# Computing the relative-position bias rows in TensorE's opening instead of behind the first chunk

## The reference

```python
for i in range(2):
    x = layer_norm(ALPHA * x + 0.5 * swiglu(x, w_gate[i, 0], w_up[i, 0], w_down[i, 0]), ...)
    m = mixer_attention(x, ...) if i == 0 else mixer_sgu(x, ...)
    x = layer_norm(ALPHA * x + m, ...)
    x = layer_norm(ALPHA * x + 0.5 * swiglu(x, w_gate[i, 1], w_up[i, 1], w_down[i, 1]), ...)
    x = x + sigmoid(x @ ple_w_gate[i]) * (p[i] @ ple_w_proj[i])
```

```python
s_own = q @ k.T * scale + rel_bias.T[head, t5_bucket(t - s)]    # 32 buckets, 8 heads; s <= t only
```

## Time and profile before

| | us |
|---|---|
| median of 3 runs | 1002.44 (1002.22 to 1002.56) |
| the profiled execution | 1002.16 |
| its span, first to last instruction | 1000.4 |
| TensorE busy | 992.9 |
| VectorE busy | 705.2 |
| ScalarE busy | 458.3 |
| GpSimd busy | 44.7 |

### The profile page before, as it was taken

How to read it: one execution, slowest core, us unless ns; L and a number is a source line. 1 busy time by engine, 2 the same in 40 slices (tenths; PEclk the granted TensorE clock), 3 DMA queues, 4 the chain that set the end, 5 groups by cost and what they waited for, 6 DMA issues and landing times.

```text
span 1000.4 us, 13938 instructions
## 1 busy us (share of the span) xinstructions
PE 992.9 (99%) x5372; PEld 849.6 (85%) x5372; DVE 705.2 (70%) x875; ACT 458.3 (46%) x523; POOL 44.7 (4%) x57
## 2 busy tenths in 40 slices
PE   9999999999999999999999999999999999999998
PEld 7888888879877888888888888888898888888887
DVE  5866666778678766666786766667787876666684
ACT  5444344246564553434355443434354553434441
POOL 0500000100001000000010000000210000000010
PEclk9999999999999999999999999999999999999999
DMA  8965656456236676565547756565467676565631
GB/s 286 286 228 170 211 171 214 131 177 201 85 127 204 217 233 213 170 213 171 175 162 254 239 173 213 169 215 175 150 191 236 212 236 214 169 213 169 215 128 43
DMA packets 129831, 191.51 MB, mean 191 GB/s; under 512 B 5464, under 2 KB 95832, under 8 KB 129792
## 3 DMA queue, kind: packets, MB, share of 16 engines
q1 hardware_dynamic: 126432, 180.11, 54.6%
q0 software_dynamic: 3072, 10.61, 3.0%
q10 hardware_dynamic: 288, 0.26, 0.1%
HBM read 189.90 MB, written 1.06 MB: 191 GB/s over the span
## 4 chain that ended last, share of the span: by engine, by line
PE 94%; DVE 3%; DMA 1%; ACT 1%; issue 0%; SPq 0%; DVEq 0%; ACTq 0%
PE gu L599 26%; PE gu L607 14%; PE acc L417 9%; PE acc L418 9%; PE acc L419 9%; PE gu L417 5%; PE gu L419 5%; PE gu L418 5%; PE tp L512 2%; PE gu L813 2%; PE gu L901 2%; DVE g_lo L1294 1%; PE gu L794 1%; PE gu L818 1%; PE gu L906 1%; DMA rawA<-in_ffn_w_up 1%
## 5 line engine op out<-in xcount | busy, mean ns | idle before, releaser
L599 PE MATMUL gu<-xT,g_hi 128*128 128x512 f32 x1152 | 274.6, 390 | 0.0
L599 PEld LDWEIGHTS gu<-xT,g_hi 128*128 128x128 f32 x1152 | 215.6, 188 | 44.4
L607 PEld LDWEIGHTS gu<-xT,g_lo 128*128 128x128 f32 x1152 | 147.7, 191 | 5.6
L1442 DVE TENSOR_REDUCE stage<-gu 128x256 f32<-128x512 f32 x72 | 49.7, 690 | 145.6 <-PE gu L607 145.6
L1294 DVE TENSOR_TENSOR g_lo<-rawA,g_hi 128x2048 fp32r<-128x2048 f32 (+2 forms) x65 | 139.6, 2150 | 17.6 <-ACT g_hi L967 17.5
L607 PE MATMUL gu<-xT,g_lo 128*128 128x256 f32 x1152 | 149.4, 283 | 0.0
L1294 DVE TENSOR_TENSOR g_lo<-rawB,g_hi 128x2048 fp32r<-128x2048 f32 (+1 forms) x64 | 138.6, 2166 | 10.6 <-ACT g_hi L967 10.5
L417 PE MATMUL acc<-d_hi,hT_hi 128*128 128x512 f32 x352 | 138.6, 394 | 0.0
L418 PE MATMUL acc<-d_lo,hT_hi 128*128 128x512 f32 x352 | 137.9, 392 | 0.0
L967 ACT ACTIVATE g_hi<-rawA 128x2048 fp32r<-128x2048 f32 (+2 forms) x66 | 118.0, 1793 | 41.9 <-DMA rawA<-in_ffn_w_up 16.3
L419 PE MATMUL acc<-d_hi,hT_lo 128*128 128x512 f32 x352 | 137.0, 389 | 0.0
(11 more groups left out here) (205 smaller groups left out, 1007.4 us busy)
## 6 DMA issues: line engine op xcount, KB each, us to landing
rawD<-in_ffn_w_down SPq DMA_DIRECT2D x44, 1024.0 KB, 5.5
rawA<-in_ffn_w_gate SPq DMA_DIRECT2D x42, 512.0 KB, 4.0
rawA<-in_ffn_w_up SPq DMA_DIRECT2D x42, 512.0 KB, 5.0
rawB<-in_ffn_w_gate SPq DMA_DIRECT2D x42, 512.0 KB, 3.9
rawB<-in_ffn_w_up SPq DMA_DIRECT2D x42, 512.0 KB, 4.9
rawA<-in_attn_w_in SPq DMA_DIRECT2D x12, 512.0 KB, 4.4
rawB<-in_attn_w_in SPq DMA_DIRECT2D x12, 512.0 KB, 4.8
rawA<-in_ple_w_gate SPq DMA_DIRECT2D x8, 512.0 KB, 4.8
```

Of the source, the lines that this page charges most:

```text
L599: pe.matmul(bank[:, :], g_hi[:, slot, b, at:at + P], xT[:, b, :, :].rearrange("p i t -> p (i t)"), start=b == 0, stop=False)
L607: done = pe.matmul(bank[:, 0:S], g_lo[:, slot, b, at:at + P], xT[:, b, 0, :], start=False, stop=b == KB - 1)
L1442: dve.tensor_reduce(gates, gu[0][:, :].rearrange("p (i t) -> p t i", i=2), AXX, ALU.add).then_inc(gate_sum, 1)
```

## The change

The product of `rel_sb` and `onehot_sb` is cut to its first 256 columns (one-hot table, matmul and the copy out of PSUM), and moved on TensorE from behind the first chunk into the opening, between `first_turn(0, 0)` and the dummies. There are three dummies there instead of four. GpSimd's wait for `high_q` ahead of the two loads is taken away, so that they follow the making of the identity directly.

```diff
-WARM = (6, 4)
+WARM = (6, 3)
...
-        onehot_sb = probs[0:BUCKETS, :, :].rearrange("p a b -> p (a b)")[:, 0:512]
+        onehot_sb = probs[0:BUCKETS, :, :].rearrange("p a b -> p (a b)")[:, 0:S]
...
             dummies(WARM[0])
             first_turn(0, 0)
+            pe.wait_ge(bias_in, 32)
+            pe.matmul(acc[1][0:HEADS, 1, 0:S], rel_sb[:, :], onehot_sb, start=True, stop=True).then_inc(bias_mm, 1)
             dummies(WARM[1])
...
-                    if k == 0:
-                        pe.wait_ge(bias_in, 32)
-                        pe.matmul(acc[1][0:HEADS, 1, :], rel_sb[:, :], onehot_sb, start=True,
-                                  stop=True).then_inc(bias_mm, 1)
                     turn(u0, t0, 0)
...
                         dve.wait_ge(bias_mm, 1)
-                        link(dve.tensor_copy(bias_row_sb, acc[1][0:HEADS, 1, :]))
+                        link(dve.tensor_copy(bias_row_sb[:, 0:S], acc[1][0:HEADS, 1, 0:S]))
                         dve.memset(bias_row_sb[:, S:512], NEG).then_inc(bias_sb, 1)
...
-            pool.wait_ge(high_q, 2)
             pool.dma_start(rel_sb[:, :], rel_bias).then_inc(bias_in, 16)
             pool.dma_start(onehot_sb, bucket_onehot).then_inc(bias_in, 16)
...
-    onehot = np.zeros((BUCKETS, 512), np.float32)
+    onehot = np.zeros((BUCKETS, S), np.float32)
```

## The result

The changed kernel takes 1003.9 us in the median of 20 executions, the kernel before 1002.38: ratio 1.0014, 95% interval [1.0008, 1.0021]. That is inside the stated range and within 0.2%, and it is slower. The median hides the most telling thing, the spread. Before lies between 1001.82 and 1002.85. The text calls these fourteen the late group.

A forecast was written before the change was run, and what follows sets the result against it. TensorE, busy 99% of the span, was taken as the bound. A chunk 1.69 us late less 0.95 saved gave +0.74: span 1000.4 + 0.7 = 1001.1, profiled execution 1002.9, median 1003.1, range 1001.9 to 1004.3.

The forecast's parts named there:

- That TensorE bounds the kernel, and that only its first 30 us matter: Whole kernel: TensorE busy 99% of the span; a shift surviving to the gapless run from 26.75 us is passed on whole.
- The cost of the old place, 0.95 us, hidden beyond 0.2 by d_lo: Behind the first chunk: moving the product frees 0.95 us; the down product's wait for d_lo lets at most 0.2 through.
- When the loads land: Opening, GpSimd's two loads: one-hot table issued at 2.25 lands 5.2 us later, at 7.45; bounds 3.3 to 5.7 us.
- L - 6.71: Net delay at TensorE's feature matmuls, with L the second load's landing time in us; never below -0.2.
- That only 0.08 us of slack lie in the first chunk: First chunk on TensorE: of the second half's turn being 1.77 late, only 0.08 us is absorbed, leaving 1.69.
- The early packets cost between -0.1 and +0.1: Opening's loads: 32 KB less and the other 32 KB 6 us earlier shift them by -0.1 to +0.1 us.
- my fourth rival: Opening: landing later than any row shows, or an early bias load delaying x_tok; 1 us more makes 1004.1; chance 0.08.
- The third rival, the clock: Opening: TensorE's clock falls during the wait for the tables, 1.53 us lost in addition, median 1004.7; chance 0.08.
- a net delay of +0.74 from the landing: TensorE's feature matmuls: chunk ends 1.69 late from the tables' landing, less 0.95 saved, so 0.74 us later.
- The signs that I had named for being right: Profile after: wait for the table until near 7.4, turn near 8.6, feature matmul near 21.6, down product 27.5 without wait.
- the first rival: Opening: loads land in time, d_lo caps the gain at 0.2 us, median about 1002.2; chance 0.25.
- the likeliest case's own range: The forecast case itself, table landing from 6.5 to 8 us: median 1002.2 to 1003.9; chance 0.55.

The follow-up runs named there:

- e2: Kernel before with only the product, table and copy halved; place, waits and four dummies kept: median 1001.84 us, 0.45 below before.
- e6: Changed kernel with the opening product on the identity, waiting for no load, tables loaded late and unread: median 1001.95 us, 0.34 below before.
- e4: Kernel before with only GpSimd's wait for high_q ahead of the two loads taken away: median 1002.87 us, 0.58 above before.
- e10: Kernel before with the product halved in its old place and both tables loaded at once: median 1002.19 us, before 1002.34.
- e1: The changed kernel timed again without any edit, eleven executions: median 1003.62 us, from 1001.61 to 1005.1.
- e5: Kernel before without its four dummies behind the first turn, no load or product moved: median 1004.48 us, from 1001.88 to 1005.38.
- e3: Changed kernel with seven dummies ahead of the wait for the tables instead of three behind the product: median 1002.28 us, from 1002.09 to 1002.64.
- e9: Kernel before with two dummies behind the first turn instead of four: median 1003.18 us.

## Why the prediction was right or wrong

*That TensorE bounds the kernel, and that only its first 30 us matter:* right. In the twelve profiles the loop is entered between 29.10 and 32.15, and from there to the end of the execution it is always 972.7 to 973.2 us.

*The cost of the old place, 0.95 us, hidden beyond 0.2 by d_lo:* right in mechanism, wrong in size. Against the same d_lo there was no slack at all: its piece starts at 24.26 and ends at 26.54 both before and after, and the loop begins at 29.49 and 29.53, although TensorE arrived 0.37 earlier after. What came through in e2 (0.45) and e6 (0.34) goes with an earlier d_lo (23.75 and 23.88 against 24.26). I had taken the end of d_lo from one profile as if it held in every execution.

*When the loads land:* the bounds (3.3 to 5.7 us) hold, the value was too late. From issue to landing the table took 4.2 and 4.5 us, not 5.2. I had L = 7.45, the product started at 6.69 and 7.02. With L - 6.71 that makes the net -0.1 and +0.3; the six undisturbed executions (1002.2) lie near that. The Trainium skill's 2.0 us of fixed cost ("DMA: Bandwidth & Descriptors", Anatomy of one DMA — SWDGE (gpsimd) path) would, as an estimate, have the table land near 4.4. It landed at about 6.6, more than 2 us later, so the rows decide against the figure for time from issue.

*That only 0.08 us of slack lie in the first chunk:* too small. The second half's turn began 1.08 us late after the change, but the turn behind the chunk 0.32 us early (20.32 against 20.64), where 1.08 - 0.08 - 0.95 would be 0.05 late. Most of the difference lies between that turn and the first product, 0.60 us before (6.83 to 7.43) and 0.35 after (7.99 to 8.34). It made no odds for the end, since d_lo took it.

*The early packets cost between -0.1 and +0.1:* too small, by the medians. They put the cost at 0.58 us for the full table and 0.35 for the half (e4, e10). I reckoned bytes over throughput; in e4's profile it is a late quarter of x that TensorE waits for, the disturbance that my fourth rival had named. e10's profile shows no such wait.

*The third rival, the clock:* I gave it 0.08, and it is what the experiments point to for the 14 late ones of 20 executions (and 7 of 11 in e1). Its price, 1.53 on top, was about right: 1.52 in e1's profile, 2.2 in e5's. What failed is the argument against it, that dummies behind the wait would guard the level and that earlier stops had done no harm. In e1 three dummies stood behind the wait, and the level fell behind them. The stops of before were short because four dummies filled them, which is exactly what the change took from in front of the stop. And that no row showed a fall proved nothing, since no row had a stop of that length. The Trainium skill ("TensorE: Matmul & The Clock Gate", Part 1: throttled by default, released by activity, taken back after idling) has both forms that the profiles show, the late rise (e5, half pace until 13) and the taking back (e1, granted 0.56 and 0.59); the traces agree with it so far.

The range around 1003.1 thus held 1003.9, but that is luck: the terms were wrongly shared out, with a net delay of +0.74 from the landing that was mostly not there, and in its place the clock. The signs that I had named for being right (the turn near 8.6, the feature matmuls near 21.6, no wait at the down product) are absent in the profile of one of the six: 7.88, 20.46, and a wait. It is close to the first rival; in the late group it is the third. The measured median sits at the very edge of the likeliest case's own range (1002.2 to 1003.9), and no single execution lies near 1003.1: they lie on both sides of it.

## What to carry to other kernels

In this kernel dummy matmuls guarded TensorE's level where they stood ahead of the wait (e3) and not behind it (e1). A gap in the opening cost nothing in one execution and 1 to 3 us in the next, so read the spread of the times, not one profile. Work taken from a full engine and put into its opening must find its operands there already, and loading them early may take time from the loads that the opening waits for (e4).

## What the runs showed of the hardware that I had not expected

- The moment at which TensorE reaches its upper level differs from execution to execution of the same opening: the first turn took 0.66 us in before's profile and 1.06, 0.77 and 1.11 in those of after, e1 and e5.
- The granted clock can read 1.00 in a stretch at half pace before the first rise (e5, products 0.43 us apart until 13 us).
- The rise can come inside the dummies: in e2 the eight passes took 1.71 us instead of 1.06 and that execution (1002.2) stayed within the narrow spread of its kernel; with none or two dummies (e5, e9) products ran at half pace until 13 and 10.8.
- 64 KB loaded by GpSimd early (issued from 1.8 us on) raised the median by 0.58 us (e4), where 370 GB/s would give 0.18; the interval of the ratio, 0.9995 to 1.0013, does not exclude no change at all.
